# SwiGLU with seven block products: copies of partial sums placed ahead of roundings, and one addition placed ahead of the next pair's weight sums

## The reference

```python
def swiglu(x, w_gate, w_up, w_down):
    return (jax.nn.silu(x @ w_gate) * (x @ w_up)) @ w_down

for i in range(DEPTH):                      # DEPTH = 2
    x = layer_norm(DN_ALPHA * x + 0.5 * swiglu(x, ffn1_w_gate[i], ffn1_w_up[i], ffn1_w_down[i]), ...)
    y = swa_mixer(...) if i == 0 else nsa_mixer(...)
    x = layer_norm(DN_ALPHA * x + y, ...)
    x = layer_norm(DN_ALPHA * x + mem_cross_attention(x, mem, ...), ...)
    x = layer_norm(DN_ALPHA * x + 0.5 * swiglu(x, ffn2_w_gate[i], ffn2_w_up[i], ffn2_w_down[i]), ...)
```

## Time and profile before

| what | value |
|---|---|
| time, median of 3 runs | 2214.04 us (2213.98 to 2214.81) |
| the profiled execution's own time | 2213.08 us |
| its span | 2210.9 us |
| mean granted PE clock | 0.995 |
| PE busy | 2172.3 us, 98% of the span |
| DVE, ACT, POOL busy | 1363.7, 1067.2, 1029.4 us |
| PE matmuls of lines 1948 to 1950 (`quarter`) | 245.2, 244.4, 244.4 us for the form bank<-x,w |

### The profile page before, as it was taken

The page is one execution under the profiler, slowest core; times in us unless marked ns, Lnnn a source line. Parts: engine busy times, 40 slices in busy tenths (PEclk is TensorE's granted clock), DMA queues, the critical chain, the costliest instruction groups (busy, mean ns, idle before and its releaser), DMA issues.

```text
span 2210.9 us, 35571 instructions
## 1 busy us (share of the span) xinstructions
PE 2172.3 (98%) x13654; PEld 1924.8 (87%) x13654; DVE 1363.7 (62%) x2239; ACT 1067.2 (48%) x1919; POOL 1029.4 (47%) x725
## 2 busy tenths in 40 slices
PE   8999999999999999999999999999999999999998
PEld 7989898878888989898899989887778888989896
DVE  7657576464436938385766666657655346848485
ACT  4435355563445525354643534467654445525353
POOL 4433336567647343335543333555548555342423
PEclk9999999999999999999999999999999999999999
DMA  4323334213313333333232333320004312333332
GB/s 150 112 95 99 103 112 134 80 49 109 121 38 106 104 96 105 97 104 126 82 119 86 101 100 120 120 77 30 20 11 130 108 54 71 111 100 94 108 96 77
DMA packets 58199, 207.50 MB, mean 94 GB/s; under 512 B 6960, under 2 KB 7088, under 8 KB 57264
## 3 DMA queue, kind: packets, MB, share of 16 engines
q1 hardware_dynamic: 56016, 197.68, 28.6%
q10 hardware_dynamic: 2016, 7.55, 0.9%
HBM read 203.10 MB, written 2.10 MB: 93 GB/s over the span
## 4 chain that ended last, share of the span: by engine, by line
PE 89%; DVE 4%; POOL 2%; ACT 2%; DMA 1%; issue 1%; ACTq 0%; DVEq 0%
PE bank L1737 14%; PE bank L1738 14%; PE bank L1739 14%; PE bank L1948 9%; PE bank L1950 9%; PE bank L1949 9%; PE bank L2147 2%; PE bank L2108 2%; PE bank L2080 1%; POOL w_lo L652 1%; DMA w_raw<-w_dram 1%; PE bank L2081 1%; DVE f L1434 1%; PE bank L1837 1%; PE bank L1838 1%
## 5 line engine op out<-in xcount | busy, mean ns | idle before, releaser
L611 POOL TENSOR_TENSOR w_lo<-w_raw,w_hi 128x1024 fp32r<-128x1024 f32 (+1 forms) x226 | 530.5, 2355 | 417.8 <-ACT w_hi L803 417.6
L652 POOL TENSOR_TENSOR w_lo<-w_raw,w_hi 128x512 fp32r<-128x512 f32 x152 | 249.2, 1660 | 532.2 <-ACT w_hi L871 532.2
L1737 PE MATMUL bank<-h_hi,w_hi 128*128 128x512 f32 x960 | 381.0, 397 | 2.5 <-DVE h_lo L1541 1.1
L1738 PE MATMUL bank<-h_lo,w_hi 128*128 128x512 f32 x960 | 374.4, 390 | 0.0
L1739 PE MATMUL bank<-h_hi,w_lo 128*128 128x512 f32 x960 | 374.0, 390 | 0.0
L803 ACT ACTIVATE w_hi<-w_raw 128x1024 fp32r<-128x1024 f32 (+1 forms) x227 | 230.7, 1021 | 130.6 <-PE bank L1739 92.3
L1948 PE MATMUL bank<-x_hi,w_hi 128*128 128x256 f32 x864 | 245.2, 284 | 0.2
L1949 PE MATMUL bank<-x_lo,w_hi 128*128 128x256 f32 x864 | 244.4, 283 | 0.0
L1950 PE MATMUL bank<-x_hi,w_lo 128*128 128x256 f32 x864 | 244.4, 283 | 0.0
L1737 PEld LDWEIGHTS bank<-h_hi,w_hi 128*128 128x128 f32 x960 | 180.4, 188 | 47.9 <-issue 4.7
L1739 PEld LDWEIGHTS bank<-h_hi,w_lo 128*128 128x128 f32 x960 | 180.2, 188 | 38.1
(11 more groups left out here) (304 smaller groups left out, 5770.1 us busy)
## 6 DMA issues: line engine op xcount, KB each, us to landing
w_raw<-w_dram SPq DMA_DIRECT2D x315, 512.0 KB, 3.5
w_raw<-w_dram SPq DMA_DIRECT2D x64, 448.0 KB, 3.3
f<-mem_dram ACTq DMA_DIRECT2D x5, 1024.0 KB, 5.3
out_dram<-t SPq DMA_DIRECT2D x8, 256.0 KB, 2.2
t<-x_dram SPq DMA_DIRECT2D x2, 512.0 KB, 6.9
f<-cmp_w_dram ACTq DMA_DIRECT2D x1, 1024.0 KB, 5.2
t<-x_dram ACTq DMA_DIRECT2D x2, 256.0 KB, 5.6
t<-x_dram ACTq DMA_DIRECT2D x1, 512.0 KB, 8.2
```

Source lines behind the costliest of these rows:

```text
L611: pool.tensor_tensor(w_lo[:, slot(s), 0:n * P], w_raw[:, s % RAW, 0:n * P], w_hi[:, slot(s), 0:n * P].bitcast(F32), ALU.subtract).then_inc ...
L652: pool.tensor_tensor(lo[:, c], raw_half(g.gate, i), hi[:, c].bitcast(F32), ALU.subtract).then_inc(gate_lo, 1)
L1737: pe.matmul(dst, w_hi[:, slot(s), w], m_hi[:, k, :], start=k == 0, stop=False)
L1738: pe.matmul(dst, w_hi[:, slot(s), w], m_lo[:, k, :], start=False, stop=False)
```

## The change

Five edits of order; no instruction is added or removed, and PE's, POOL's and SP's programs stay as they are.

1. ACT, once a SwiGLU: `keep1(begin)` goes ahead of `comb_round(1, 0)` and `up_round(begin)`.
2. ACT, once a SwiGLU: `keep3(begin)` goes from the start of the second pair's turn to the place between the two `pair_round` of the second pair.
3. DVE, once a SwiGLU: `pair_rest(begin, 0)` goes ahead of `whole(2)`.
4. DVE, in all pairs but `begin`, which is 72 times: `first(g)` goes ahead of `sums_first(g.next)`. In the last pair of a part nothing comes between, so it moves in 60 of them.
5. What follows from 2: `keep3` and `keep1` of `begin` are left out at their old places.

```diff
@@ scalar engine, ffn
                 pair_round(begin, 1)
                 hi(2, 0)
+                keep1(begin)
                 act.wait_ge(slab_done, plain(st.s0 + 5))
                 comb_round(1, 0)
                 up_round(begin)
@@
                     for g in mine:
-                        if before:
+                        if before and before is not begin:
                             keep3(before)
-                        keep1(g)
+                        if g is not begin:
+                            keep1(g)
                         if g.next:
                             gate_round(g.next)
@@
                         if g.next:
                             pair_round(g.next, 0)
+                            if g is begin:
+                                keep3(g)
                             pair_round(g.next, 1)
@@ vector engine, ffn
                 comb_rest(4, 2)
+                pair_rest(begin, 0)
                 whole(2)
-                pair_rest(begin, 0)
                 pair_rest(begin, 1)
@@
                         if before:
                             up2(before)
+                        if g is not begin:
+                            first(g)
                         if g.next:
                             sums_first(g.next)
-                        if g is not begin:
-                            first(g)
                         if g.next:
                             sums_second(g.next)
```

## The result

The changed kernel took 2225.07 us (median of four runs, 2222.64 to 2226.65) against 2214.01 (2213.97 to 2214.81) for the kernel before. The ratio is 1.005, its 95% interval 1.0037 to 1.0062: slower, by 11.1 us. The forecast was 2223.8, from a sum of +10.3. The profiled execution took 2223.99 us with a span of 2221.9.

The account below looks back on a forecast made before the run. PE, busy 98%, was taken as the bound, with the third copy's chain at nearly its pace behind it. Later parts +7.0 and +1.9, first parts +2.2 and -0.8 gave +10.3, so 2223.8 us; 8 in 10 range 2206 to 2230.

Parts of the forecast that it names:

- What bounds the kernel: PE is busy for 98% of the span; behind its waits the third copy's chain runs at 10.09 us against PE's 10.11.
- The collision keeps going: Later parts: DVE's sum L1434 no longer slips ahead of POOL, so 0.31 us a pair is lost as collisions go on.
- Rival D: A collision holds DVE for a whole half of POOL's work, 1.27 us; a pair takes 10.76, time 2237; chance 0.02.
- `first` adds 0.33 to the chain: Pairs with first ahead of the sums: its 0.33 us, no longer hidden behind POOL, takes the chain from 10.09 to 10.42.
- Later parts, +7.0 and +1.9: Seven later parts lose 1.0 us each, +7.0; the eighth, which had no wait for first, loses 1.9.
- starts the second turn's sums when a transfer lands: Later parts, second turn: a transfer issued at 149.2 takes 3.5 and lands at 152.7; from there the sums meet POOL, 4.09.
- First parts: SwiGLU two to four lose 0.75 us each, +2.2 for three; the first gains, -0.8, with no clock drop expected.
- the list of what would show the theory right: Later parts: product three waits 0.2 to 0.3, distance 10.4, sums 1.4 to 1.8; begin's product one 0.4 late; no clock drop.
- The sum: Whole kernel: 7.0 + 1.9 + 2.2 - 0.8 = +10.3 us, given as 2223.8.
- Rival A: Waits go and the chain keeps its pace, L1434 getting ahead of POOL in most turns: -6.0, so 2208; chance 0.22.
- B: The chain loses 0.31 in a pair or two of each part, then gets past POOL: 2214, give or take 2; chance 0.14.

Follow-up runs that it names:

- `first` twice: The whole change with one more addition like first right ahead of it in every pair but begin; 2236.84 us, one run.
- edit 4 alone: The kernel before with only first moved ahead of the sums, the other edits undone; 2226.41 us, ratio 1.0056.
- `first` behind the third sum: The whole change, but first goes behind the third of the next pair's four sums, ahead of the fourth; 2209.50 us, ratio 0.9984.
- edits 1 to 3: The whole change with DVE's order in the pairs put back as in the kernel before; 2211.85 us, ratio 0.9989.
- edits 1 and 2: The kernel before with only the two copies of begin moved; pair_rest(begin, 0) stays behind whole(2); 2213.21 us, one run.

## Why the prediction was right, and where it was off

**What bounds the kernel.** Right. The chain behind the third copy is what PE meets next, and its pace with `first` in front is 10.42, as given. PE's own pace is 10.08, where the forecast read 10.11 from a turn that was not yet steady: a pair costs 0.33 and not 0.31.

**The collision keeps going.** Right, and now tested from three sides: L1438 and L1443 take 1.78 in the steady turns, and moving POOL, emptying it, or letting the sums pass ahead of it each brings back 10.08. Rival D (1.27 a collision) is out: L1438 is held for 1.78 - 0.68 = 1.10. By the Trainium skill's page ("SBUF — State Buffer", section "SBUF: two separate sides") the loser stands for the whole instruction. The trace is nearer to that than 1.27 against 1.10 looks. In the run with `first` twice POOL starts a half at 173.68, which alone takes 1.27 and so ends near 174.95; L1436 asks at 173.87 and has run 0.68 when it ends at 175.52, so it got through at 174.84, 0.1 before that end. The hold is shorter than the half because DVE asks after POOL has started, and by this 0.1. For the sum the measured 1.10 decides.

**`first` adds 0.33 to the chain.** Right for this turn, wrong as a rule, as the run with `first` twice shows (0.19 for the second 0.33).

**Later parts, +7.0 and +1.9.** Measured +10.3 in sum. For the part I worked out it is 74.88 - 73.81 = +1.07 against +1.0: the step from product to product fits within 0.05 (third copy done 10.36 us behind the part's start by the forecast, 10.37 in the trace; second product three 21.05 and 21.04). One term between the two had the wrong cause, though. The forecast starts the second turn's sums when a transfer lands, 11.7 behind the part's start. They start at 11.7, but behind no transfer:

```profile
151.55 0.42 DVE L1462 TENSOR_TENSOR f<-mkf,bank 128x256 f32<-128x256 f32 x1
151.88 1.79 DVE L1436 TENSOR_TENSOR f<-w_raw 128x512 f32<-128x512 f32 x1
```

DVE is busy up to L1436. In the kernel before it stood for a transfer at this place in all eight later parts, 13.1 us in sum; with the change in one, for 0.3. That DVE's own work reaches L1436 at the same moment is luck. The slip in size is that I took this part for all seven. In the six others product seven's wait for `first` had been 0.15 shorter and the part lasted 73.67 (one 73.69), so they lost 1.2 each, 0.8 more in sum. The eighth lost 2.01.

**First parts.** First SwiGLU: -0.78 against -0.8. The clock stays up there. Windows of the changed kernel:

```profile
57.00:60.00 3.00, 3.00 (x28) 3.00 (x26) 3.00 (x3) 0.34 (x1) 2.19 (x2) 1.00 0.62 169
```

In SwiGLU two to four the parts are 0.3 longer and product one is 0.5 late: +0.8 each, +2.5 for +2.2. Timeline of PE, second SwiGLU: product one, three, six, two, three.

```profile
732.80 0.36 PE L1952 MATMUL bank<-x_hi,w_hi 128*128 128x256 f32 x1 [0.35 <-POOL w_lo L652]
...
743.59 0.39 PE L1952 MATMUL bank<-x_hi,mv 128*128 128x256 f32 x1 [0.49 <-ACT mkf L902]
...
745.64 0.39 PE L1952 MATMUL bank<-ra,w_hi 128*128 128x256 f32 x1 [0.35 <-ACT mkf L894]
...
754.22 0.38 PE L1952 MATMUL bank<-x_hi,w_hi 128*128 128x256 f32 x1 [1.13 <-DVE f L1396]
...
755.98 0.39 PE L1952 MATMUL bank<-x_hi,w_hi 128*128 128x256 f32 x1
```

The forecast had all of the second turn's lateness at product three. Most of it shows earlier: product six of the second pair starts 0.5 late for the first copy, and product two of the third pair waits 1.1 for `hid`. Products two and three hang on the same DVE operations, so the sum did not suffer, but the list of what would show the theory right did not have this wait, the largest of the new ones.

**The sum.** 10.3 (later) + 0.2 (first) + 0.5 (product one, third SwiGLU) + 0.6 and -0.6 (the stretches in front of the second and fourth, the lateness of 0.5 in each among them) is 11.0; the profiled executions differ by 10.9. That 10.3 came so near 11.0 is in part luck. The parts with their late product ones add up to 12.0, 10.3 + 1.7 where the forecast had 8.9 + 1.4, and about 1 us went the other way in the long stretches, which the change does not touch. **Rival A** failed on what was said against it, 0.33 being more than both margins. **B** did not come about, because no later part got past POOL again.

## What to carry to other kernels

Where two engines that hold each other up are released at nearly the same moment, look at what each has queued: an operation moved in front of a row of such instructions can push the row into the other engine's way. Here an addition of 0.33 us, moved forward, made a turn 0.33 longer, and it did so only because two collisions of 1.10 had brought the chain up to PE's pace; without them a turn stays at 10.08 with the addition in the same place. When a wait is removed, compare the pace of the chain behind it with that of the bound engine, to the hundredth; equal paces mean that the gain is not there. The cure was to let the sums go ahead of the release, or to hold the other engine until they are done.

## What was not expected

- **The clock drop is not tied to one wait alone.** PE stood 2.2 us for the third copy four times in the kernel before and the clock fell behind it once; in the run of edit 4 alone the same four waits brought four drops, and with `first` behind the third sum four waits of 2.3 brought one. A drop made its part 1.0 to 1.4 us longer. In no first part whose longest wait was under 2 us did it fall. What decides between one and four was not found.
- **It is also the noise.** Windows over the whole span show such drops at other places that the change does not touch: the kernel before near 1480 and 1842 us, the change near 1850 alone, edits 1 to 3 near 1479 and 1841, behind the third sum near 1477. That is the likely reason why runs of one kernel lie up to 5.5 us apart (2208.1 to 2213.6 over ten of edits 1 to 3). It was read from the profiled executions only, so it is argued, not shown, for the others.
- **A transfer's phase moves whole waits.** In the run of edits 1 and 2 one later part, behind a first part that was 0.4 later, had no wait for `first` at all and lasted 72.56, where its equals lasted 73.65 to 73.67. DVE stood for the transfer in its second turn for 0.29 us, in an equal part for 2.20. In the kernel before this same part had been the one without the wait (72.87).
